# Two unused buffers shift the addresses of the activations' high and low parts in a two-model transformer block kernel

## The reference

```python
# first model, one layer
h = rms_norm(x, g);  proj = h @ w_in                       # 1024 -> 8192
ya = moba_attention(...); yb = rg_lru(...) * gelu(rgate); yc = diff_attention(...)
merged = g0 * (ya @ w_branch_a) + g1 * (yb @ w_branch_b) + g2 * (yc @ w_branch_c)
x = x + merged @ w_out
u = causal_dwconv(rms_norm(x) @ ffn_up)                    # 1024 -> 5632
x = x + (gelu(u_gate) * u_val) @ ffn_down                  # 2816 -> 1024
x = rms_norm(x)
# second model, two layers: pooling, grouped attention, a gated convolution
proj = x @ w_in                                            # 1024 -> 4864
merged = sum of three gated branches (each y @ w_branch);  x = layer_norm(a * x + merged @ w_o)
x = layer_norm(a * x + (silu(u_gate) * u_val) @ w_down)    # up 1024 -> 5632, down 2816 -> 1024
```

## The kernel before, in words

| buffers | start modulo 512 before | after |
|---|---|---|
| raw, whi, wlo | 0 | 0 |
| xhi, xlo, yhi, ylo, x, rgw, poolw, const, prob, probT, table, rope_cs, tmp, acc | 0 | 448 |
| ones, ipos, soft | 32 | 480 |
| lamdot; vec; small | 192; 448; 64 | 128; 384; 0 |
| u1, u2, fhi, flo, dev, ugate, uval, fprod, pads, zpad | 448 | 448 |

## Time and profile before

### The profile page before, as it was taken

How to read it: one execution, slowest core, us unless ns; L and a number is a source line. 1 busy time by engine, 2 the same in 40 slices (tenths; PEclk the granted TensorE clock), 3 DMA queues, 4 the chain that set the end, 5 groups by cost and what they waited for, 6 DMA issues and landing times.

```text
span 1348.4 us, 26782 instructions
## 1 busy us (share of the span) xinstructions
PE 1258.8 (93%) x9986; PEld 1216.0 (90%) x9986; DVE 892.9 (66%) x1469; ACT 715.2 (53%) x1235; POOL 362.0 (27%) x351
## 2 busy tenths in 40 slices
PE   5999889799899999899998999998999988999996
PEld 4988779799899999898997999998988987999996
DVE  5656667566677755665577777756655577777755
ACT  4554558344566654455544666543555444666643
POOL 2020100712243411130035343413120045343313
PEclk9999989999899999899999899999899998999998
DMA  6633334455455656444545455665444544456563
GB/s 236 184 114 111 101 119 128 140 194 180 129 186 184 186 176 197 138 149 126 153 161 156 133 181 184 182 181 169 130 138 138 158 157 126 158 185 182 158 209 93
DMA packets 60286, 212.67 MB, mean 158 GB/s; under 512 B 6688, under 2 KB 7968, under 8 KB 60064
## 3 DMA queue, kind: packets, MB, share of 16 engines
q1 hardware_dynamic: 60192, 211.39, 50.4%
HBM read 210.31 MB, written 1.05 MB: 157 GB/s over the span
## 4 chain that ended last, share of the span: by engine, by line
PE 75%; DVE 8%; issue 6%; POOL 6%; ACT 4%; DMA 0%; POOLq 0%; DVEq 0%; SPq 0%; ACTq 0%
PE bank L985 24%; PE bank L987 23%; PE bank L986 23%; POOL acc L602 2%; DVE wlo L1240 2%; ACT whi L668 1%; POOL u L589 1%; PE bank L1105 1%; POOL u L551 1%; PE bank L1016 1%; PE bank L1079 1%; PE bank L1078 1%; PE bank L1088 1%; DVE dev L1259 1%; PE bank L1127 1%
## 5 line engine op out<-in xcount | busy, mean ns | idle before, releaser
L985 PE MATMUL bank<-xhi,whi 128*128 128x256 f32 x2368 | 692.0, 292 | 38.3 <-DVE xlo L1244 16.7
L1240 DVE TENSOR_TENSOR wlo<-raw,whi 128x1024 fp32r<-128x1024 f32 (+1 forms) x400 | 501.1, 1254 | 280.7 <-ACT whi L668 277.9
L986 PE MATMUL bank<-xlo,whi 128*128 128x256 f32 x2368 | 677.1, 286 | 0.0
L987 PE MATMUL bank<-xhi,wlo 128*128 128x256 f32 x2368 | 676.8, 286 | 0.0
L985 PEld LDWEIGHTS bank<-xhi,whi 128*128 128x128 f32 x2368 | 461.0, 195 | 59.5 <-issue 48.6
L668 ACT ACTIVATE whi<-raw 128x1024 fp32r<-128x1024 f32 (+1 forms) x400 | 414.8, 1039 | 144.3 <-PE bank L987 130.3
L986 PEld LDWEIGHTS bank<-xlo,whi 128*128 128x128 f32 x2368 | 461.9, 195 | 0.7
L987 PEld LDWEIGHTS bank<-xhi,wlo 128*128 128x128 f32 x2368 | 461.3, 195 | 0.0
L575 POOL TENSOR_TENSOR fprod<-ugate,uval 128x256 f32<-128x256 f32 x66 | 88.4, 1340 | 239.0 <-DVE uval L1576 217.8
L985 PE MATMUL bank<-fhi,whi 128*128 128x256 f32 x528 | 146.6, 278 | 4.2 <-DVE wlo L1240 4.2
L987 PE MATMUL bank<-fhi,wlo 128*128 128x256 f32 x528 | 145.9, 276 | 0.0
(11 more groups left out here) (197 smaller groups left out, 1249.4 us busy)
## 6 DMA issues: line engine op xcount, KB each, us to landing
raw<-in_w_win SPq DMA_DIRECT2D x140, 512.0 KB, 3.5
raw<-in_w_up SPq DMA_DIRECT2D x132, 512.0 KB, 3.5
raw<-in_w_down SPq DMA_DIRECT2D x48, 448.0 KB, 3.8
raw<-in_w_merge SPq DMA_DIRECT2D x32, 512.0 KB, 4.0
raw<-in_w_out SPq DMA_DIRECT2D x24, 512.0 KB, 3.5
raw<-in_w_down SPq DMA_DIRECT2D x24, 512.0 KB, 3.6
x<-in_x SPq DMA_DIRECT2D x4, 256.0 KB, 4.6
rgw<-in_rg_w SPq DMA_DIRECT2D x1, 1024.0 KB, 10.4
```

The lines of the kernel that those rows point to most:

```text
L985: pe.matmul(ps, whi[:, slot, w], hi, start=first, stop=False)
L986: pe.matmul(ps, whi[:, slot, w], lo, start=False, stop=False)
L987: return pe.matmul(ps, wlo[:, slot, w], hi, start=False, stop=last)
L1240: dve.tensor_tensor(wlo[:, n % RING, w], raw[:, n % RING, w], whi[:, n % RING, w].bitcast(f32), ALU.subtract) \
```

## The change

Two buffers are allocated that nothing reads or writes: 112 float32 values (448 bytes of each partition) between `wlo` and `xhi`, and 16 values (64 bytes) after `small`. Everything from `xhi` to `small` moves up by 448 bytes, and everything from `u1` on by 512. Every instruction stays, in the same order, with the same shapes and waits.

```diff
         raw = sb("raw", [P, RING, 8 * P])
         whi = sb("whi", [P, RING, 8 * P], r32)
         wlo = sb("wlo", [P, RING, 8 * P], r32)
+        sb("line_x", [P, 112])
         xhi = sb("xhi", [P, KT, S], r32)
         xlo = sb("xlo", [P, KT, S], r32)
         yhi = sb("yhi", [P, 16, S], r32)
@@
         small = sb("small", [P, 96])
 
+        sb("line_u", [P, 16])
         with ExitStack() as one:
             u1 = sb("u1", [P, 72, S], stack=one)
```

## The result

| | before | after |
|---|---|---|
| median of four executions each, same chip | 1351.16 us (1350.68 to 1352.32) | 1332.02 us (1331.54 to 1334.80) |
| ratio | | 0.9863, 95% interval 0.9851 to 0.9875 |
| span of the profiled execution | 1348.4 us | 1330.6 us |
| mean granted TensorE clock | 0.975 | 0.969 |

The kernel is faster by 19.1 us. The forecast was 41.8 us, and 1332.0 lies outside the range of 1301 to 1326. The sign and the place of the gain were right, the size was not.

What follows compares the result with a forecast made beforehand. TensorE's matmuls, slowed where weight load and moving read share an offset, were taken as the bound: 52.5 us gain less 3.5 and 7.2 leaves 41.8, so 1351.1 - 41.8 = 1309.3 us, range 1301 to 1326.

Steps and rivals of the forecast that it cites:

- No change: Rival: f is faster for its far place, so x and y stay at 120.0 ns; 1351 us, chance 0.10.
- At the two prices a unit takes 2.88 or 2.72 us: Products with x and y: each of 328 units of 24 matmuls gains 0.16 us, 52.5 us in all.
- a remainder of 1.0 us: Products just behind a break: some matmuls already start 116 to 117 ns apart, so 1.0 us of gain is taken off.
- the forecast's own share of 41.8 in 52.5: Whole kernel: of 52.5 us gained in the products, 41.8 us shows in the time after deductions of 3.5 and 7.2.
- `f` stays at 448: Down products: f keeps its offset of 448 modulo 512, and 24 of its matmuls still take 2.72 us.
- at 7 ns to either side: Small matmuls, under 530 of 9986: at most 3.7 us either way, mostly hidden by waits; taken as zero.
- Part (a): Product matmuls not at 120 ns now: 372 gain nothing, 2.5 us; with 1.0 us for quicker ones, 3.5 us.
- The clock term: Lower-clock stretches of 3 to 6 us may fall elsewhere; two more or two fewer are 2.4 us either way.
- The bounds 1301 and 1320: Forecast's own range: 1301 with nothing hidden, clock and small matmuls in favour; 1320 with twice as much hidden, the rest against.
- Slower: Rival: among near places 448 is a bad offset, x goes to 123.3 ns; 23 us lost, 1374 us, chance 0.04.
- Part (b): Units where TensorE does not set the pace (differential heads, scan, second model's merges, long waits): 7.2 us of gain hidden.
- Half a gain: Rival: x near the weights settles at 116.7 ns, giving half of 41.8 us; 1330 us, chance 0.04.

Runs made afterwards that it cites:

- the repeated kernel: The changed kernel run once more unaltered for a second profile, against the kernel before: 1333.89 us, ratio 0.9869.
- the map: Kernels with x, y and f at further distances from the weights, against the kernel before: 1330.68, 1351.19, 1356.03, 1360.08 and 1360.91 us.

## Why the prediction failed, and where it held

**The diagnosis held.** That the pace depends on the distance of the two operands in their low address bits is shown by the weights' move, where it changed with `x` left in place, from 119.85 to 116.28 ns. That the two reads delay each other is an inference of mine; no run shows the delay itself. The longer weight loads that the prediction took as its sign are none in general: with `x` at distance 184 matmuls also stand at 120.0 ns, and the loads take 188 or 190 ns. The rival *No change*, by which the far place made `f` fast, falls: `x`, which lies near, has 138 units at 113.3 ns at 448, and 139 at 192. Whether another engine's access ever delays TensorE these runs do not show, beyond ScalarE's writes to `whi` and VectorE's to `wlo`, with which the distance stayed at 120.0 ns.

**The step that failed** is the first of the sum: "At the two prices a unit takes 2.88 or 2.72 us", 328 units at 0.16. I took 2.72 for the price of place 448, since all 72 units of `f` had it. It is one of two steady paces of that place, and which of them a stretch gets is settled at its last disturbance. `f` has few: 24 units in a row, with one small step in two of the down products, and that step left 113.3 behind with `ones` at 32. `x` has one at nearly every unit of the input products and some in the up products, where every turn behind the 5th unit was one to 117.8, except behind an added transpose. The rows that warned were there: the earlier trace rows has distances of 116 to 117 ns behind a break, and I read them as a remainder of 1.0 us instead of asking how long a pace lasts and who sets it.

An estimate from the paces: `x` (115.75 - 113.3) x 7104 = 17.4 us and `y` (116.97 - 113.3) x 768 = 2.8 us. If the forecast's own share of 41.8 in 52.5 shows in the time, that is 16.1 us.

**"`f` stays at 448"**, and so at its price, was the second half of the same step. 48 of its 72 units went to 117.8: 1584 x (116.32 - 113.42) = 4.6 us, 4.2 in the phases. The change moved `ones`, and 40 of the 48 stand behind its matmul; the other 8 are six of the eight ahead of it and the first two of the first model's. I had priced the small matmuls, "at 7 ns to either side", for their own duration alone. What they cost is what they leave behind: 20 units.

**Part (a), 2.5 us.** That 372 matmuls gain nothing was my estimate, and no run shows the term as such. What the two profiles show is that the long distances stayed: at a granted clock of 0.50 the median distance of `x` was 214 ns before and 213 after, and at 1.00 the distances between 126 and 400 ns ahead of a matmul of `x` or `y` had a median of 223 ns before (166 of them) and 222 after (186).

**The clock term** named what came and was too small. I gave two stretches more or fewer, 2.4 us. The changed kernel has 12 stretches with a granted clock of 0.50, 83.1 us, where the kernel before had 9 with 66.5. They hold some 42 more matmuls at 213 ns: 42 x 96 ns = 4.0 us. The window of the earlier trace rows in the changed kernel and the one of its differential heads, which had 0.96 in the earlier trace rows:

```profile
124.00:165.00 41.00, 34.77 (x226) 31.24 (x227) 26.25 (x80) 20.21 (x54) 5.85 (x5) 0.88 0.28 91
190.00:196.00 6.00, 5.53 (x22) 5.20 (x23) 4.80 (x6) 3.45 (x7) 0.00 (x0) 0.50 0.55 158
```

Two stretches with a granted clock of 0.50, 10.2 us, became four with 23.8 us in the input product of the first model, and its length fell by 1.35 us instead of 7. In the repeated kernel it fell by 3.25 us, so part of this is that one execution. That a quicker product sends TensorE there more often is only likely: the repeated kernel had 11 such stretches in 83.5 us.

41.8 - 16.1 - 4.6 - 4.0 = 17.1 us, and the span fell by 17.8. Nothing large is left over, but the share that shows was assumed and not measured.

**Sums that do not come out.** The bounds 1301 and 1320 are not what their words add up to: nothing hidden, with the clock and the small matmuls in favour, is 1309.3 - 7.2 - 2.4 - 3.7 = 1296.0 us, and the rest all against is 1309.3 + 7.2 + 2.4 + 3.7 + 1.4 = 1324.0. The measured 1332.0 lies outside these as well. In *Slower*, the share that (a) and (b) leave of 26 us is 21 and not 23.

**Part (b), the covered units, held.** In the scan the wait for ScalarE took up what the products gave, and its units kept their length. TensorE's timeline in the changed kernel (start us, us, idle before):

```profile
250.38 0.36 PE L987 MATMUL bank<-xhi,whi 128*128 128x256 f32 x1 [1.51 <-ACT u L861]
...
254.87 0.36 PE L987 MATMUL bank<-xhi,whi 128*128 128x256 f32 x1 [1.42 <-ACT u L861]
...
259.35 0.36 PE L987 MATMUL bank<-xhi,whi 128*128 128x256 f32 x1 [1.51 <-ACT u L861]
```

A unit still takes 4.48 us, as in the earlier trace rows. The second model's merges went from 24.53 to 24.16 and from 24.52 to 23.87 us. The waits of TensorE after, against the earlier trace rows:

```profile
PE bank L987 <- ACT u L861: 10.7, 7, 3.0
...
PE bank L1129 <- ACT tmp L800: 6.6, 1, 6.6
...
PE bank L1080 <- DVE small L1410: 5.4, 4, 1.5
...
PE bank L987 <- ACT u L970: 3.8, 2, 1.9
```

They grew by 0.2 to 0.3 us each, so no new bound took the gain. The vector engines' new offsets cost nothing that shows (VectorE 892.9 to 883.3 us busy, ScalarE 715.2 to 716.0).

**The rivals.** *Half a gain* named about the time that came, 1330 us, by "settles at the value of those breaks", and had 0.04. That is luck in the number, since its mechanism was wrong: the mean of `x` is 115.75 ns, between the two paces, and not a pace of its own. *Slower* needed 448 to be above 120.0; it isn't, and in the map only 200 is, by 0.1 ns.

**What stays open.** Why 192 modulo 256 is the good distance, why it has two paces and why the up products fall to the slower one was not found. What picks between them behind a wait is not known. No layout tried kept `x` at 113.3, so the forecast's 1309 was not reached by any kernel; the best median is 1327.77 us.

## What to carry to other kernels

Where TensorE streams matmuls with a weight load each (here float32r with 256 columns), the distance between the stationary and the moving operand's SBUF addresses modulo 256 was worth up to 6% of a matmul's pace (113.3 against 120.0 ns) and 1.7% of this kernel's time, and the pads cost 512 bytes of each partition: try several, and move only the operands of the products, high and low parts alike, leaving those of the small matmuls where they were. Read the pace as distances between starts over whole phases and behind every kind of restart, since one operand's steady pace in one phase doesn't tell that another operand gets it at the same address. A one-matmul step between two streams is to be priced by the pace that it leaves behind, not by its own duration.

## What the runs showed of the hardware

- A stream of matmuls with 256 columns, three to a block of weights and each with its own weight load, ran at 113.3 to 120.1 ns per matmul at a granted clock of 1.00, by the distance of the two operands modulo 256. At a granted clock of 0.50 the median distance of `x` was 213 or 214 ns in every profile, with `x` at 0, 64, 96, 176, 184, 192 or 224 modulo 256 from the weights.
- At distance 192 modulo 256 there were two steady paces, 113.3 and 117.8 ns (24 matmuls in 2.72 and 2.82 us), kept over tens of units and changed from one to the other only at a longer distance, of which the shortest read was 141 ns. At distance 64 most units ran at 117.8 and 15 at 113.3.
- At 117.8 with distance 192 one weight load in three takes some 192 ns and the others 188 (71 of 213 long loads from 405 to 430 us in the changed kernel), at 120.0 with distance 0 all take some 192 in a steady stretch, at 113.3 all 188. At distance 184 the pace is 120.0 too; with `x` there the loads take 188 or 190 ns, with `f` there 191.
- In the down products one matmul decided the pace of the 20 units behind it by the place of its stationary operand: 113.3 ns with it at 32 or 288 modulo 512, 117.8 with it at 480 or 256, without exception in twelve profiles. In the output products the same step had 2 exceptions in 20.
